# Two transformer blocks on one core: another order of work at four waits of TensorE, and the last norm by halves of the tokens

## The reference

```python
# first block, layer 0 and layer 1
x = x + rglru_mixer(rms_norm(x, norm_mix_g[0]), ...)   # gate and branch, conv, two gates, scan, (h * gelu(gate)) @ rec_w_out
x = x + sq_relu_mlp(rms_norm(x, norm_mlp_g[0]), ...)   # square(relu(h @ w_up)) @ w_down, 4096 wide
x = x + dsa_mixer(rms_norm(x, norm_mix_g[1]), ...)     # index scores, top-128 keys, attention over a latent
x = x + sq_relu_mlp(rms_norm(x, norm_mlp_g[1]), ...)
x = rms_norm(x, final_norm_g)
# second block
h = rmsnorm(x, norm_mix)                               # second norm of a row of two: sums of squares of both
q, k, v, r, lr_f, lr_b, u, g_a, g_b = split(h @ w_in)
o = gla(q, k, v, decays of lr_f) + gla(reversed, decays of lr_b)      # 4 heads, chunks of 64
o = normed(o) * gla_norm * silu(r)
merged = sigmoid(g_a) * (o @ w_branch_gla) + sigmoid(g_b) * pooled(u)
x = x + merged @ w_out
gate, up = split(rmsnorm(x, norm_ffn) @ w_ffn_in)      # 2816 wide
x = x + (silu(gate) * up) @ w_ffn_out
return rmsnorm(x, norm_final)
```

## Time and profile before

| | us |
|---|---|
| time, median of 3 runs | 1879.57 (1879.13 to 1879.93) |
| the profiled execution | 1879.85 |
| its span | 1878.6 |
| PE busy | 1859.6 (99%) |
| DVE busy | 977.0 (52%) |
| ACT busy | 674.3 (36%) |
| POOL busy | 379.9 (20%) |
| HBM traffic | 172.36 MB in all, 91 GB/s over the span |
| TensorE's granted clock, mean | 0.999 of full speed |

### The profile page before, as it was taken

How to read it: one execution, slowest core, us unless ns; L and a number is a source line. 1 busy time by engine, 2 the same in 40 slices (tenths; PEclk the granted TensorE clock), 3 DMA queues, 4 the chain that set the end, 5 groups by cost and what they waited for, 6 DMA issues and landing times.

```text
span 1878.6 us, 21854 instructions
## 1 busy us (share of the span) xinstructions
PE 1859.6 (99%) x8896; PEld 1505.6 (80%) x8900; DVE 977.0 (52%) x1318; ACT 674.3 (36%) x912; POOL 379.9 (20%) x339
## 2 busy tenths in 40 slices
PE   9999999999999999999999999999999999999998
PEld 8888888888877568888888878788787888888887
DVE  7885533334458864543434347666446454443432
ACT  6753322222234772321212334555323332222213
POOL 2004210010336793210101131111001311110103
PEclk9999999999999999999999999999999999999999
DMA  4323322322322103223223222222232322233221
GB/s 159 113 90 90 112 90 93 109 90 91 107 96 93 66 1 112 90 90 112 90 91 111 76 91 90 68 68 68 84 117 79 112 88 93 90 101 101 90 95 62
DMA packets 167171, 172.36 MB, mean 92 GB/s; under 512 B 7480, under 2 KB 164288, under 8 KB 167072
## 3 DMA queue, kind: packets, MB, share of 16 engines
q1 hardware_dynamic: 164576, 163.76, 26.9%
q0 software_dynamic: 2496, 7.21, 1.2%
HBM read 168.69 MB, written 2.14 MB: 91 GB/s over the span
## 4 chain that ended last, share of the span: by engine, by line
PE 86%; DVE 6%; ACT 4%; issue 2%; DMA 0%; POOL 0%; SPq 0%; DVEq 0%; ACTq 0%
PE bank L775 27%; PE bank L777 27%; PE bank L776 27%; DVE wlo L1700 1%; DVE XC L1802 1%; PE bank L800 1%; ACT whi L1218 1%; PE bank L994 1%; PE bank L1096 1%; PE bank L973 1%; ACT pt L1438 0%; PE bank L922 0%; DVE qe L2106 0%; DMA xtok<-in_x 0%; PE bank L1163 0%
## 5 line engine op out<-in xcount | busy, mean ns | idle before, releaser
L775 PE MATMUL bank<-Ahi,whi 128*128 128x512 f32 (+2 forms) x1416 | 552.8, 390 | 2.5 <-DVE wlo L1700 0.8
L776 PE MATMUL bank<-Alo,whi 128*128 128x512 f32 (+2 forms) x1416 | 547.8, 387 | 0.0
L777 PE MATMUL bank<-Ahi,wlo 128*128 128x512 f32 (+2 forms) x1416 | 547.8, 387 | 0.0
L1700 DVE TENSOR_TENSOR wlo<-stage,whi 128x2048 fp32r<-128x2048 f32 (+2 forms) x146 | 333.1, 2281 | 380.3 <-ACT whi L1218 380.3
L1218 ACT ACTIVATE whi<-stage 128x2048 fp32r<-128x2048 f32 (+2 forms) x152 | 287.1, 1889 | 443.3 <-PE bank L777 443.3
L775 PEld LDWEIGHTS bank<-Ahi,whi 128*128 128x128 f32 (+1 forms) x1416 | 265.3, 187 | 65.6 <-issue 8.2
L776 PEld LDWEIGHTS bank<-Alo,whi 128*128 128x128 f32 (+1 forms) x1416 | 265.4, 187 | 54.9 <-issue 1.2
L777 PEld LDWEIGHTS bank<-Ahi,wlo 128*128 128x128 f32 (+1 forms) x1416 | 265.3, 187 | 55.0
L775 PE MATMUL bank<-Hhi,whi 128*128 128x512 f32 x688 | 267.7, 389 | 0.0
L777 PE MATMUL bank<-Hhi,wlo 128*128 128x512 f32 x688 | 267.6, 389 | 0.0
L776 PE MATMUL bank<-Hlo,whi 128*128 128x512 f32 x688 | 267.6, 389 | 0.0
(11 more groups left out here) (349 smaller groups left out, 2145.4 us busy)
## 6 DMA issues: line engine op xcount, KB each, us to landing
stage<-in_mlp_w_up SPq DMA_DIRECT2D x32, 1024.0 KB, 5.3
stage<-in_mlp_w_down SPq DMA_DIRECT2D x32, 1024.0 KB, 4.9
stage<-in_w_in SPq DMA_DIRECT2D x22, 1024.0 KB, 4.9
stage<-in_w_ffn_in SPq DMA_DIRECT2D x22, 1024.0 KB, 4.9
stage<-in_w_ffn_out SPq DMA_DIRECT2D x8, 1024.0 KB, 5.0
stage<-in_rec_w_in SPq DMA_DIRECT2D x7, 1024.0 KB, 5.1
stage<-in_att_w_in SPq DMA_DIRECT2D x6, 1024.0 KB, 5.3
stage<-in_rec_w_out SPq DMA_DIRECT2D x4, 1024.0 KB, 4.6
```

What stands on the lines that cost most here:

```text
L775: e.matmul(ps, hi, rh, start=first, stop=False)
L776: e.matmul(ps, hi, rl, start=False, stop=False)
L777: return e.matmul(ps, lo, rh, start=False, stop=last)
L1700: e.tensor_tensor(lo_of(u)[:, 0:nk, 0:n], stage[s][:, 0:nk, 0:n], f32(hi_of(u)[:, 0:nk, 0:n]), ALU.subtract).then_inc(s_lo[s], 1)
```

## The change

The arithmetic is the same but for the order of a sum: the squares of the last two tiles are no longer summed with the others, but enter TensorE's sum by themselves. Six edits:
1. Start, DVE: the low half of the first 128 columns (L1735) is made before `copy_x(1)`.
2. DVE: `lo(11)` is made behind `scan(7)`, before `mix(6)`, `y_low(5)` and `gate_out(7)`.
3. PE: the sums of squares "ss", "ss2" stand between "qk0" and "qk2" instead of behind "qk2"; in the ring too.
4. PE: `turn_outputs(h-1)` stands between the products r(2h) and r(2h+1), for h = 1 to 3; the ring gets r(2h) before the two "on" labels. DVE scales r(2h) first, then gated and gated_lo, then scales r(2h+1).
5. First FFN unit: the high half of the third unit is made by ACT before the two tanh, and its low half by DVE between the first scale_out and its gating.
6. The end: fd(2,6) and fd(2,7) are computed as products of 256 tokens, halves 0 and 1, with transposes and sums between them; DVE makes the squares of tiles 6 and 7 by halves (POOL those of the six others); root, reciprocal, scaled copies and output DMAs run for the first 256 tokens and then for the last. The sums go to banks 6 and 7.

The diff; of long runs of removed lines, which stand in the kernel above, the first and the last are kept.

```diff
@@ -316,8 +316,8 @@
         u_end["wo", m] = ("wo", 2 * m + 1)
     ring_mlp(1)
     pair("lr", "lr")
-    pair(("Q", 0), ("qk", 0), ("qk", 2))
-    ring.add("ss", "ss2")
+    ring.add(("qk", 0), "ss", "ss2")
+    pair(("Q", 0), ("qk", 2))
     pair(("K", 0), ("qk", 1), ("qk", 3))
     ring.add("rt", ("z", 0, 0), ("z", 0, 1))
     pair(("V", 0), ("v", 0, 0), ("v", 0, 1))
@@ -327,8 +327,8 @@
         if h == 0:
             pair(("Q", 1), ("qk", 4), ("qk", 6))
         else:
-            ring.add(("on", h - 1, 0), ("on", h - 1, 1))
-            pair(("R", h), ("r", 2 * h), ("r", 2 * h + 1))
+            ring.add(("r", 2 * h), ("on", h - 1, 0), ("on", h - 1, 1))
+            pair(("R", h), ("r", 2 * h + 1))
         between = ("R", 0) if h == 0 else ("GA", h - 1)
         for g in range(2):
             ring.add(*[("kv", h, g, d, par) for d in range(2) for par in range(2)])
@@ -365,8 +365,8 @@
         if g < 2:
             ring_ffn(g + 1)
             blocks(("fd", g), 8)
-    blocks(("fd", 2), 7)
-    ring.add(*[("y", 0, j) for j in range(4)], ("fd", 2, 7), *[("y", 1, j) for j in range(4)], "rt2")
+    blocks(("fd", 2), 6)
+    ring.add(*[("y", 0, j) for j in range(4)], ("fd", 2, 6), ("fd", 2, 7), *[("y", 1, j) for j in range(4)])
     u_end["fd", 2, 3] = ("fd", 2, 7)
     ends = [u_end[label] for label, u in sorted(u_of.items(), key=lambda x: x[1])]
 
...
@@ -755,7 +756,7 @@
                 e.wait_ge(s_fgate, n + 1)
                 e.tensor_tensor(fu[n % 4][:, :], fu[n % 4][:, :], fg[n % 4][:, :], ALU.mult).then_inc(s_fu, 1)
         e.wait_ge(*ring.free("root_f"))
-        for m in range(7):
+        for m in range(6):
             square("out", m, ring.free(("fd", 2, m)))
 
 
@@ -1038,12 +1039,12 @@
         product("lr", s, 0, Ahi, Alo, width=96, ready=s_alo, n0=FILL["gla"])
         s = take_unit(("Q", 0))
         product(("qk", 0), s, 0, Ahi, Alo)
-        product(("qk", 2), s, 128, Ahi, Alo)
         ps = begin("ss")
         e.wait_ge(s_tsp, 14)
         e.matmul(ps[:, :], ones[:, :], sqa[:, :], start=True, stop=True).then_inc(*ring.put("ss"))
         ps = begin("ss2")
         e.matmul(ps[:, :], ones[:, :], sqb[:, :], start=True, stop=True).then_inc(*ring.put("ss2"))
+        product(("qk", 2), s, 128, Ahi, Alo)
         s = take_unit(("K", 0))
         product(("qk", 1), s, 0, Ahi, Alo)
         product(("qk", 3), s, 128, Ahi, Alo)
@@ -1131,9 +1132,9 @@
                 product(("qk", 4), s, 0, Ahi, Alo)
                 product(("qk", 6), s, 128, Ahi, Alo)
             else:
-                turn_outputs(h - 1)
                 s = take_unit(("R", h))
                 product(("r", 2 * h), s, 0, Ahi, Alo)
+                turn_outputs(h - 1)
                 product(("r", 2 * h + 1), s, 128, Ahi, Alo)
             states(h, 0)
             s = take_unit(("R", 0) if h == 0 else ("GA", h - 1))
@@ -1180,30 +1181,65 @@
         for g in range(2):
             ffn_up(g + 1)
             gemm(("fd", g), 8, Hhi[g % 2], Hlo[g % 2], s_hlo, 64 + FG[g][0], nk=FG[g][1])
-        gemm(("fd", 2), 7, Hhi[0], Hlo[0], s_hlo, 64 + FG[2][0], nk=FG[2][1])
+        gemm(("fd", 2), 6, Hhi[0], Hlo[0], s_hlo, 64 + FG[2][0], nk=FG[2][1])
         for j in range(4):
             ps = begin(("y", 0, j))
             for c in range(4):
                 e.wait_ge(s_y, c + 1)
                 t = e.transpose(ps[:, c * 128:(c + 1) * 128], Y[:, c, j * 128:(j + 1) * 128], ident[:, :])
             t.then_inc(*ring.put(("y", 0, j)))
-        product(("fd", 2, 7), u_of["fd", 2, 3], 128, Hhi[0], Hlo[0], nk=FG[2][1])
-        for c in range(4, 7):
+
+        def last_product(m, half):
+
+            label, s, cols = ("fd", 2, m), u_of["fd", 2, 3], slice(256 * half, 256 * half + 256)
+            ps = ring.bank(label) if half else begin(label)
+            w = slice((m - 6) * 128, (m - 5) * 128)
+            for k in range(FG[2][1]):
+                i = three(ps[:, cols], hi_of(s)[:, k, w], lo_of(s)[:, k, w], Hhi[0][:, k, cols], Hlo[0][:, k, cols], k == 0, k == FG[2][1] - 1)
+            i.then_inc(s_fh, 1)
+
+        def turn_y(c, j):
+            ps = begin(("y", 1, j)) if c == 4 else ring.bank(("y", 1, j))
+            return e.transpose(ps[:, (c - 4) * 128:(c - 3) * 128], Y[:, c, j * 128:(j + 1) * 128], ident[:, :])
+
+        def sums(half, square_of, first):
+
+            for j in (2 * half, 2 * half + 1):
+                t = e.matmul(banks[6 + half][:, j % 2:j % 2 + 1], square_of[:, j * 128:(j + 1) * 128], ones[:, 0:1],
+                             start=first and j % 2 == 0, stop=square_of is sqb and j % 2 == 1)
+            return t
+
+        take_unit(("fd", 2, 3))
+        last_product(6, 0)
+        last_product(7, 0)
+        for c in (4, 5):
+            e.wait_ge(s_y, c + 1)
             for j in range(4):
-                ps = begin(("y", 1, j)) if c == 4 else ring.bank(("y", 1, j))
...
-        t.then_inc(*ring.put("rt2"))
+                turn_y(c, j)
+        e.wait_ge(s_y, 7)
+        for j in (0, 1):
+            turn_y(6, j)
+        last_product(6, 1)
+        e.wait_ge(s_sq, SQ["out"] + 6)
+        sums(0, sqa, True)
+        e.wait_ge(s_sqh, 2)
+        sums(0, sqt2, False)
+        sums(0, sqb, False).then_inc(s_rts, 1)
         e.wait_ge(s_y, 8)
-        for j in range(4):
-            e.transpose(ring.bank(("y", 1, j))[:, 384:512], Y[:, 7, j * 128:(j + 1) * 128], ident[:, :]).then_inc(*ring.put(("y", 1, j)))
+        for j in (0, 1):
+            turn_y(7, j).then_inc(*ring.put(("y", 1, j)))
+        sums(1, sqa, True)
+        last_product(7, 1)
+        e.wait_ge(s_y, 9)
+        for j in (2, 3):
+            turn_y(6, j)
+        e.wait_ge(s_sqh, 3)
+        sums(1, sqt2, False)
+        e.wait_ge(s_sqh, 4)
+        sums(1, sqb, False).then_inc(s_rts, 1)
+        e.wait_ge(s_y, 10)
+        for j in (2, 3):
+            turn_y(7, j).then_inc(*ring.put(("y", 1, j)))
 
 
     def scalar_program(e):
@@ -1649,11 +1685,13 @@
                 hi(u_of["fg", g, j] + 1)
                 if g == 0 and j == 0:
                     std_of("root_f", 1024)
+                    hi(u_of["fu", g, j] + 1)
                 for i in range(2):
                     n = fcount[g, j + i]
                     e.wait_ge(*ring.free(("fg", g, j + i)))
                     e.activation(ft[n % 4][:, :], fg[n % 4][:, :], ACT.Tanh, scale=0.5).then_inc(s_ft, 1)
-                hi(u_of["fu", g, j] + 1)
+                if g or j:
+                    hi(u_of["fu", g, j] + 1)
                 for i in range(2):
                     n = fcount[g, j + i]
                     e.wait_ge(s_fu, n + 1)
@@ -1665,27 +1703,41 @@
         for g in range(3):
             if g < 2:
                 ffn_up(g + 1)
-            for what, m in product_order(8):
-                if what == "w" and u_of["fd", g, m] + 1 < len(units):
+            for what, m in product_order(8 if g < 2 else 6):
+                if what == "w":
                     hi(u_of["fd", g, m] + 1)
                 if what == "e" and g == 2:
                     e.wait_ge(*ring.free(("fd", g, m)))
                     if m == 0:
                         e.wait_ge(*ring.full(("fu", 2, 5)))
                     e.activation(Y[:, m, :], X[:, m, :], ACT.Identity, scale=c2("fin2", m)).then_inc(s_y, 1)
-                    if m == 6:
...
-        e.wait_ge(s_rtok, 1)
         for j in range(4):
-            label = ("y", 1, j)
+            label = ("y", 0, j)
             e.wait_ge(*ring.full(label))
-            e.activation(YT[:, j, 512:1024], ring.bank(label)[:, :], ACT.Copy, scale=rtok[:, j:j + 1]).then_inc(*ring.take(label))
+            e.activation(YT[:, j, 0:512], ring.bank(label)[:, :], ACT.Copy).then_inc(*ring.take(label))
+        e.activation(oss[:, 7:8], epsc[:, 0:1], ACT.Sqrt).then_inc(*st.inc())
+
+        def scaled_y(n, m, half):
+            cols = slice(256 * half, 256 * half + 256)
+            e.wait_ge(s_xh, n)
+            e.activation(Y[:, m, cols], X[:, m, cols], ACT.Identity, scale=c2("fin2", m)).then_inc(s_y, 1)
+
+        def normed(half):
+            j2 = slice(2 * half, 2 * half + 2)
+            e.wait_ge(s_rts, half + 1)
+            e.activation(rtok[:, j2], banks[6 + half][:, 0:2], ACT.Sqrt, bias=epsc[:, 0:1], scale=1.0 / 1024).then_inc(s_last, 1)
+            e.wait_ge(s_rtok, half + 1)
+            for j in (2 * half, 2 * half + 1):
+                label = ("y", 1, j)
+                e.wait_ge(*ring.full(label))
+                e.activation(YT[:, j, 512:1024], ring.bank(label)[:, :], ACT.Copy, scale=rtok[:, j:j + 1]).then_inc(*ring.take(label))
+
+        scaled_y(1, 6, 0)
+        scaled_y(2, 7, 0)
+        scaled_y(3, 6, 1)
+        normed(0)
+        scaled_y(4, 7, 1)
+        normed(1)
 
 
     def vector_program(e):
@@ -1730,9 +1782,9 @@
         copy_x(0)
         e.wait_ge(*ring.full("v0"))
         e.tensor_copy(cols0[:, :], ring.bank("v0")[:, 0:16]).then_inc(*ring.take("v0"))
-        copy_x(1)
         e.wait_ge(s_hi_a, 1)
```

(45 more changed lines are left out.)

28 lines of the change are left out of this document (4 added, 24 removed).

## The result

The changed kernel took 1874.85 on the median of ten runs (1874.16 to 1875.25), the kernel before 1879.72 in the same session (1879.03 to 1880.27): 4.87 less, a ratio of 0.9975 with an interval of 0.9966 to 0.9983. Forecast were 1875.3 and 4.3 less. The profiled execution took 1874.16 with a span of 1872.8.

The account below looks back on a forecast made before the run. TensorE, busy 99%, bounds the kernel, so reordering wins only at its pauses or behind its last matmul. 0.34 + 0.97 + 1.00 + 0.84 + 1.02 + 0.15 = 4.32 off 1879.85: 1875.53, or 1875.3 median; range 1873.6 to 1877.3.

Parts of the forecast that it names:

- Parts 1, 2, 3 and 5: PE's pauses at the start, lo(11), the sums of squares and the first FFN unit: 0.34, 0.97, 1.00 and 1.02 gained.
- The cover that I named for each: Work delayed by the reordering is wanted late enough, e.g. 5.4 later at lo(11), a unit (10.9) at the first FFN unit.
- the 0.4 at which I had called myself wrong: Sign in the list of PE's waits: a new line over 0.4 there would show the forecast wrong.
- the doubt: Sums of squares ahead of qk2: POOL's squares might not be there 5.4 earlier, so lower bound 0.3 against 1.00.
- Rival A: Turned outputs: their wait goes whole, as though r's product found a free bank; 2.3 in all, 1873.0; chance 0.07.
- Part 4's size: Turned outputs, three heads: 0.4 at h=1 and 0.2 each at h=2 and 3, sum 0.84, bounds 0 and 1.4.
- Part 6: The end by halves: reciprocal 2.35 later against two transfers of 1.25 fewer, 0.15 gained; bounds 0.9 gained, 1.0 lost.
- two transfers fewer: The end: only two output DMAs are left behind the last sums instead of four, each transfer worth 1.25.
- Rival B: The end: short matmuls and more handovers cost 0.7 to 2, so 1876.2 to 1877.5; chance 0.14.
- C: Attention: pauses for POOL's scalings grow as PE comes earlier, giving gains back; 1876.6 to 1878; chance 0.06.
- Rival D: The end: PE's clock falls to 1.2 GHz around the moved transposes and short matmuls, up to 1889; chance 0.03.
- the line of 0.2%: Whole kernel: what can be told from no change, 3.76, so 1875.81; the forecast lay 0.5 better.

## Why the prediction was right, point by point

- **What bounds the kernel.** "Matmuls set the time, an order can win only where PE stands" held: PE's busy time moved by 0.2, and the span by the pauses.
- **Parts 1, 2, 3 and 5**, priced as idle + 0.16 + 0.11, came out at 0.32, 0.99, 1.05 and 1.04 against 0.34, 0.97, 1.00 and 1.02. With those parts undone the pauses are back and nothing else has moved, so they are causes, not neighbours. At the start PE's own pause is no steady measure, since it moves with the input: it is 0.48 and 0.49 in two traces with part 1 in, gone in others, and was 0.52 before. What part 1 does is steady: PE's second product begins 2.35 to 2.36 behind the start of ACT's high half in the eleven traces with part 1 in which that low half came last, and 2.68 to 2.69 in the two without, the 0.34 of the working. The cover that I named for each held: no new line stands in PE's list but the one at the end. That one is 0.41 by its row, a hair over the 0.4 at which I had called myself wrong; but the working itself has PE stand there (last product to 1871.55, squares to 1872.5), so the sign was badly set and not the mechanism. For part 3 the doubt was POOL's squares; the sums ran without a wait.
- **Part 4's reason** was the one bold step: r(2h) takes the place of the turned output in the row of banks, so its wait stays. It is shown by three runs, from both sides: another bank lengthens the wait by 0.59, an earlier release of this one shortens it by 0.70, and undoing the part puts the same 1.3 back at the transposes. Rival A (1873.0) fell with it.
- **Part 4's size** was low, 1.08 instead of 0.84, and the mis-sized term is the pauses around the transposes. I counted them as idle time plus 0.16, the overlap of matmuls of 512 columns. Eight transposes overlap more with what follows: in the changed kernel their row is 1.04 long and the product behind it starts after 0.79 (1208.02, 1208.81). Before, that distance was 1.39 at head 1 (1205.66 to 1207.05) and 1.19 at head 2 (1253.75 to 1254.94 above). So 0.60 and 0.39 went, not 0.5 and 0.32. The restart that I took off is real: r(2h) and r(2h+1) now both stand behind transposes, where only r(2h) did, and the first matmul there is 0.47 to 0.48 long with or without a wait (1202.45, 1208.81 above). With 0.08 to 0.12 for it the rows give 0.48 and 0.30, and 0.46 and 0.31 were measured.
- **Part 6** was forecast at 0.15 and the traces show 0.46. In the clock of before, PE's rows came where the working put them: half products from 1859.40 (1859.4), their end at 1863.79 (1863.8), the last product's end at 1871.15 (1871.4) and the reciprocal at 1873.23 (1873.5). The term that was mis-sized there is the small steps ahead of that product's end, 0.25 in all: three calls of sums took 1.26 (1861.70 to 1862.96) and not 1.4, and the rest are roundings upward of 0.05 to 0.1 each; behind it every step is as computed, and the 0.3 stay to the last landing: the third DMA leaves 2.06 behind the first one's time of before (2.3 forecast), and the span ends 3.95 behind it (3.9). The term "two transfers fewer" is shown by the held DMAs, 2.52 for two. What I had missed is that the time outside the span grows by 0.13, so that the time gains less than the trace; and the times themselves, of nineteen and twenty runs, show no gain of part 6 at all.
- **Rival B** (the end costs) and **C** (gains given back in the attention) didn't come: the shift ahead of and behind the attention differs by 0.01 in 985 us, and the times leave no room for the 0.7 that B would have cost.
- **Rival D**, the clock, was wrong in its mechanism, as 96 transposes show. The clock did fall in this case, but elsewhere: in two executions, 1.2 and 1.7 behind the end of a pause of PE. There it cost 1.6 where it could be read, not the 4.3 and more that D needed.
- **The chances.** The forecast lay 0.5 beyond the line of 0.2%, and the result 0.45 beyond that. That extra is no merit of the forecast: parts 4 and 6 were both low, by 0.24 and 0.31, and 0.1 went back outside the span. The interval reaches from 0.17% to 0.34%: that the kernel is faster is shown, that it is so by more than 0.2% is likely.

## What to carry to other kernels

When a product is moved into a wait, look up which buffer it gets there: with banks handed out in a fixed row, it inherits the wait together with the place, and the cure here was an earlier release (0.7) and then an earlier input (0.9 more), not another order of the waiter. A removed pause is worth its idle time plus the overlap and the restart (take the overlap from rows of the same kind: 0.16 for the long matmuls, 0.25 for eight transposes), but for every place ask what is late next, since at two of three heads here it was so close behind that 0.06 to 0.08 came of an expected 0.24. For parts of under 0.5 the shift between traces decides and medians of ten runs don't; add what lies outside the span, which the trace doesn't show.
